# Modulation tiles of the first block as whole 128x2048 tiles in two neighbouring slots of the weight ring

## What is computed

```
mod = silu(c) @ w_mod + b_mod
shift, scale, gate = split(mod, 3)
h = rms_norm(x, g_pre) * (1 + scale) + shift
proj = h @ w_in
y = concat(attention, spatial gating, gated linear attention) * silu(z)
out = y @ w_out
x = x + gate * rms_norm(out, g_post)
```

## Time and profile before

| | |
|---|---|
| median of three runs | 2891.63 us |
| the profiled execution, its own time | 2893.03 us |
| span of its profile, first to last instruction | 2891.3 us |
| first block, about | 0 to 890 us |
| late modulation tiles on VectorE | 163 to 776 us |
| mean granted TensorE clock | 0.985 |
| TensorE busy | 2792.5 us (97%) |
| VectorE busy | 1792.4 us (62%) |
| ScalarE busy | 1375.3 us (48%) |
| late modulation transfers | 79 + 49 = 128 of 512 KB |

### The profile page before, as it was taken

The page is one execution under the profiler, slowest core; times in us unless marked ns, Lnnn a source line. Parts: engine busy times, 40 slices in busy tenths (PEclk is TensorE's granted clock), DMA queues, the critical chain, the costliest instruction groups (busy, mean ns, idle before and its releaser), DMA issues.

```text
span 2891.3 us, 35716 instructions
## 1 busy us (share of the span) xinstructions
PE 2792.5 (97%) x13338; PEld 2316.7 (80%) x13338; DVE 1792.4 (62%) x2196; ACT 1375.3 (48%) x1782; POOL 36.1 (1%) x69
## 2 busy tenths in 40 slices
PE   5799998999998999999999999999999999999998
PEld 4578786888887888888888888878888888888886
DVE  6889898768755565555445556575555545445565
ACT  4355445555544444453545444444545445545443
POOL 0000000000000000000000000000000000000000
PEclk8899999999999999999999999999999999999999
DMA  9977698875564555576555565645555765555664
GB/s 394 359 274 262 203 348 302 318 231 191 188 206 151 175 175 175 163 225 193 180 177 169 174 198 190 225 160 174 175 175 165 227 190 175 175 176 177 194 217 146
DMA packets 160199, 605.16 MB, mean 209 GB/s; under 512 B 18376, under 2 KB 18560, under 8 KB 154544
## 3 DMA queue, kind: packets, MB, share of 16 engines
q1 hardware_dynamic: 155376, 583.08, 60.3%
q0 software_dynamic: 4672, 19.98, 2.1%
HBM read 600.85 MB, written 2.14 MB: 209 GB/s over the span
## 4 chain that ended last, share of the span: by engine, by line
PE 67%; DVE 1%; DMA 0%; ACT 0%; issue 0%; SPq 0%; ACTq 0%; DVEq 0%
PE acc L780 62%; PE psT L728 2%; PE psS L761 1%; PE psS L751 1%; PE psT L734 1%; PE psS L768 0%; DMA raw<-in_w 0%; DVE wlo L434 0%; ACT whi L317 0%; DVE stage L543 0%; DVE x L487 0%; PE psT L724 0%; DVE stage L532 0%; DVE x L486 0%; DVE x L468 0%
## 5 line engine op out<-in xcount | busy, mean ns | idle before, releaser
L434 DVE TENSOR_TENSOR wlo<-raw,whi 128x1024 fp32r<-128x1024 f32 x672 | 822.4, 1225 | 867.6 <-ACT whi L317 866.0
L317 ACT ACTIVATE whi<-raw 128x1024 fp32r<-128x1024 f32 x672 | 711.2, 1059 | 996.5 <-PE acc L780 980.8
L780 PE MATMUL acc<-whi,xhi 128*128 128x512 f32 x2304 | 638.4, 398 | 2.4 <-DVE xlo L440 1.5
L780 PE MATMUL acc<-whi,xlo 128*128 128x512 f32 x2304 | 619.9, 390 | 0.0
L780 PE MATMUL acc<-wlo,xhi 128*128 128x512 f32 x2304 | 619.7, 390 | 0.0
L780 PEld LDWEIGHTS acc<-whi,xlo 128*128 128x128 f32 x2304 | 433.3, 188 | 92.5
L780 PEld LDWEIGHTS acc<-wlo,xhi 128*128 128x128 f32 x2304 | 433.3, 188 | 91.7
L780 PEld LDWEIGHTS acc<-whi,xhi 128*128 128x128 f32 x2304 | 423.5, 189 | 83.2 <-DVE xlo L440 3.0
L1412 ACT ACTIVATE whi<-raw 128x1024 fp32r<-128x1024 f32 x177 | 187.2, 1059 | 270.1 <-PE acc L2163 164.3
L2163 PE MATMUL acc<-whi,hhi 128*128 128x512 f32 x864 | 250.2, 412 | 40.7 <-DVE hlo L1645 40.7
L1634 DVE TENSOR_TENSOR wlo<-raw,whi 128x1024 fp32r<-128x1024 f32 x177 | 215.2, 1222 | 89.0 <-ACT whi L1412 88.0
(11 more groups left out here) (320 smaller groups left out, 2126.6 us busy)
## 6 DMA issues: line engine op xcount, KB each, us to landing
raw<-in_w SPq DMA_DIRECT2D x849, 512.0 KB, 3.5
raw<-in_w_late SPq DMA_DIRECT2D x79, 512.0 KB, 5.1
mraw<-in_w SPq DMA_DIRECT2D x63, 512.0 KB, 4.8
mraw<-in_w_late SPq DMA_DIRECT2D x49, 512.0 KB, 4.9
b_y<-in_w_early SPq DMA_DIRECT2D x12, 1024.0 KB, 10.8
mraw<-in_w_early SPq DMA_DIRECT2D x7, 1024.0 KB, 10.6
scr<-in_w_early SPq DMA_DIRECT2D x7, 1024.0 KB, 11.8
sgl<-in_w_early SPq DMA_DIRECT2D x6, 1024.0 KB, 13.6
```

The lines of the kernel that those rows point to most:

```text
L317: act.activation(whi[:, n % SLOTS, :], raw[:, n % SLOTS, :], ACT.Copy).then_inc(s_hi, 1)
L434: dve.tensor_tensor(wlo[:, n % SLOTS, :], raw[:, n % SLOTS, :], whi[:, n % SLOTS, :].bitcast(F32), ALU.subtract).then_inc(s_lo, 1)
L780: m = pe.matmul(acc[c % 2][:, tb, :], a[:, kk, tb * P:(tb + 1) * P], b[:, n % SLOTS, k * CW:(k + 1) * CW], start=(kk == 0 and q == 0), sto ...
```

## The change

- A late modulation tile is whole: 128x2048, 1 MB, one transfer and one VectorE sum. There are 64 instead of 128. `summed` is gone, `mcol` loses its last axis, and `mraw` keeps its size.
- In the ring such a tile takes two neighbouring slots. `ring_places()` gives each item its first slot, the count of its first slot's uses, and the item that was last in the top one of its slots. SyncE waits for that one. Weights still take one slot. A tile starts at an even slot, so an even number of weights lies between two tiles.
- `late_steps()` now has, in layer 0, the odd steps from 33 on but 63, 71, 77 and 119; in layer 1 steps 3, 5, ... 17 and then 21, 25, ... 81.
- R_GATE stays 68 in layer 0 and goes from 85 to 83 in layer 1.

```diff
-LATE = [(0, 2, kt, half) for kt in range(KT) for half in range(2)]
-LATE += [(1, third, kt, half) for kt in range(KT) for third in range(2) for half in range(2)]
-LATE += [(1, 2, kt, half) for kt in range(KT) for half in range(2)]
+LATE = [(0, 2, kt) for kt in range(KT)]
+LATE += [(1, third, kt) for kt in range(KT) for third in range(2)]
+LATE += [(1, 2, kt) for kt in range(KT)]
-R_FULL = (62, 63, 64, 70, 71, 77, 99, 119)
+R_FULL = (63, 71, 77, 119)
...
-    steps = [(0, r) for r in range(R_RING, GRAN1) if r not in R_FULL]
-    steps += [(1, 1 + i) for i in range(16)]
-    steps += [(1, 21 + 2 * i) for i in range(32)]
+    steps = [(0, r) for r in range(R_RING + 1, GRAN1, 2) if r not in R_FULL]
+    steps += [(1, 3 + 2 * i) for i in range(8)]
+    steps += [(1, 21 + 4 * i) for i in range(16)]
...
-R_GATE = [[r for (layer, r), i in LATE_AT.items() if i == GATED[l]][0] + 2 for l in range(DEPTH)]
+R_GATE = [[r for (layer, r), i in LATE_AT.items() if i == GATED[l]][0] + 3 - l for l in range(DEPTH)]
...
+def ring_places():
+    places, last, uses = {}, {}, [R_RING // SLOTS if i < SLOTS else 0 for i in range(RING)]
+    at_slot = 0
+    for item in ITEMS:
+        first, width = at_slot % RING, ring_width(item)
+        assert first % width == 0
+        uses[first] += 1
+        places[item] = first, uses[first], last.get(first + width - 1)
+        for i in range(first, first + width):
+            last[i] = item
+        at_slot += width
+    return places, last
...
-            if k >= RING:
-                sp.wait_ge(*consumed(ITEMS[k - RING]))
+            if before:
+                sp.wait_ge(*consumed(before))
...
-            _, third, kt, part = LATE[i]
+            _, third, kt = LATE[i]
             dve.wait_ge(*landed(("m", i)))
-            dve.scalar_tensor_tensor(out=slot(("m", i)), in0=slot(("m", i)), scalar=1.0,
-                                     in1=crow[:, part * MOD_W:(part + 1) * MOD_W], op0=ALU.mult, op1=ALU.mult,
-                                     accum_out=mcol[:, third, kt, part:part + 1]).then_inc(s_macc, 1)
+            dve.scalar_tensor_tensor(out=slot(("m", i)), in0=slot(("m", i)), scalar=1.0, in1=crow[:], op0=ALU.mult,
+                                     op1=ALU.mult, accum_out=mcol[:, third, kt:kt + 1]).then_inc(s_macc, 1)
...
-                summed(0, kts)
-                summed(1, kts)
```

More of the change, by code:

```diff
@@ L997, in ring_items, with ring_width @@
     return out
+def ring_width(item):
+    return 2 if item[0] == "m" else 1
+def ring_places():
[10 more added lines that the diff above has]
+    return places, last
 ITEMS = ring_items()
-ITEM = {item: k for k, item in enumerate(ITEMS)}
+PLACES, LAST_USE = ring_places()
 def ring_slot(item):
-    if item in ITEM:
-        return ITEM[item] % RING
-    return item[1] % SLOTS
+    return PLACES[item][0] if item in PLACES else item[1] % SLOTS
 def ring_uses(item):
-    if item in ITEM:
-        return ITEM[item] // RING + 1 + (R_RING // SLOTS if ITEM[item] % RING < SLOTS else 0)
-    return item[1] // SLOTS + 1
+    return PLACES[item][1] if item in PLACES else item[1] // SLOTS + 1
 def h_fill(l, r):
@@ L1103, in first_block @@
     crow = sb("crow", [P, D])
-    mraw = sb("mraw", [P, 2, MOD_W])
+    mraw = sb("mraw", [P, 2, GK * CW])
     gain = sb("gain", [P, D])
@@ L1130, in first_block @@
     sinks = sb("sinks", [P, A_HEADS])
-    mcol = sb("mcol", [P, 3, KT, 2])
+    mcol = sb("mcol", [P, 3, KT])
     mbias = sb("mbias", [P, DEPTH, 3, KT])
@@ L1300, in slot @@
     def slot(item):
-        i = ring_slot(item)
-        return raw[:, i, :] if i < SLOTS else mraw[:, i - SLOTS, :]
+        i, width = ring_slot(item), ring_width(item)
+        tile = raw[:, i:i + width, :] if i < SLOTS else mraw[:, i - SLOTS:i - SLOTS + width, :]
+        return tile.rearrange("p a n -> p (a n)")
     def landed(item):
@@ L1326, in weights, with item @@
             sp.dma_start(slot(("w", n)), dram["w1"][n]).then_inc(s_w[n % SLOTS], 16)
-        def item(k):
-            kind, i = ITEMS[k]
-            if k >= RING:
-                sp.wait_ge(*consumed(ITEMS[k - RING]))
-            elif k < SLOTS:
-                sp.wait_ge(*split(R_RING - SLOTS + k))
+        def item(name):
+            kind, i = name
+            first, _, before = PLACES[name]
+            top = first + ring_width(name) - 1
+            if before:
+                sp.wait_ge(*consumed(before))
+            elif top < SLOTS:
+                sp.wait_ge(*split(R_RING - SLOTS + top))
             else:
@@ L1337, in item @@
             src = dram["w1"][i] if kind == "w" else dram["w_late"][i]
-            sp.dma_start(slot(ITEMS[k]), src).then_inc(s_w[k % RING], 16)
+            sp.dma_start(slot(name), src).then_inc(s_w[first], 16)
         for tb in range(TB):
@@ L1353, in _ @@
                 weights(n)
-        for k in range(len(ITEMS)):
-            item(k)
+        for name in ITEMS:
+            item(name)
         for n in range(SLOTS if s_next else 0):
-            sp.wait_ge(*consumed(ITEMS[max(k for k in range(len(ITEMS)) if k % RING == n)]))
+            sp.wait_ge(*consumed(LAST_USE[n]))
             sp.dma_start(raw[:, n, :], dram["w"][n]).then_inc(s_next[n], 16)
@@ L1652, in tile @@
             dve.scalar_tensor_tensor(out=big[n % len(big)], in0=big[n % len(big)], scalar=1.0, in1=crow[:], op0=ALU.mult,
-                                     op1=ALU.mult, accum_out=mcol[:, third, kt, 0:1]).then_inc(s_macc, 1)
+                                     op1=ALU.mult, accum_out=mcol[:, third, kt:kt + 1]).then_inc(s_macc, 1)
         def late(i):
-            _, third, kt, part = LATE[i]
+            _, third, kt = LATE[i]
             dve.wait_ge(*landed(("m", i)))
-            dve.scalar_tensor_tensor(out=slot(("m", i)), in0=slot(("m", i)), scalar=1.0,
-                                     in1=crow[:, part * MOD_W:(part + 1) * MOD_W], op0=ALU.mult, op1=ALU.mult,
-                                     accum_out=mcol[:, third, kt, part:part + 1]).then_inc(s_macc, 1)
-        def summed(third, kts):
-            link(dve.tensor_tensor(mcol[:, third, kts, 0], mcol[:, third, kts, 0], mcol[:, third, kts, 1], ALU.add))
+            dve.scalar_tensor_tensor(out=slot(("m", i)), in0=slot(("m", i)), scalar=1.0, in1=crow[:], op0=ALU.mult,
+                                     op1=ALU.mult, accum_out=mcol[:, third, kt:kt + 1]).then_inc(s_macc, 1)
         def columns_of(l, j):
@@ L2213, in modulation_stream @@
     w = w_mod.reshape(DEPTH, D, 3, KT, P).transpose(0, 2, 3, 4, 1)
-    late = [w[l, third, kt, :, part * MOD_W:(part + 1) * MOD_W] for l, third, kt, part in LATE]
+    late = [w[l, third, kt] for l, third, kt in LATE]
     return {"w_early": np.ascontiguousarray(w[0, 0:2]), "w_late": np.stack(late)}
```

8 lines of the change are left out of this document (3 added, 5 removed).

## The result

The changed kernel takes **2905.44 us** (median of six runs, 2900.48 to 2913.2), the kernel before beside it 2891.51 us (six runs, 2889.99 to 2893.78). The ratio is 1.0048, 95% interval 1.0038 to 1.0059: slower by 11 to 17 us, where 2891.6 us and a range up to 2898 had been forecast. The profiled execution is 2908.0 us with a span of 2906.3 us.

The account below looks back on a forecast made before the run. TensorE was taken to bound the first block, hiding VectorE and transfers behind its weight lead. Every term was worth 0, so the profiled 2893.03 us stayed the same; for the median, 2891.6 us, range 2888.5 to 2898.

Parts of the forecast that it names:

- What bounds the kernel: First block: TensorE bound wherever late modulation tiles lie; smallest weight lead 1.70 us, at granule 97 of layer 0.
- Order in the ring: Granules 96 and 97, layer 0: paired weight requests shift the lead, 2.9 us more to 3.1 less; no stall taken.
- The loop: Rival: ring closes too slowly between granules 96 and 118; 2895 to 2904 us, most likely 2898; chance 0.15.
- Transfers: Modulation tiles in the ring: same bytes in 64 fewer pieces, rate margin from about 1% to 9%; worth 0.
- The rival by which the rows are cut into the same pieces: Transfers stay at 388 GB/s, time as forecast; no chance of its own, within the 0.79 shared with forecast and small stalls.
- A blocking sum: VectorE's 2.29 us sum delays the even granule's `lo`, but `wlo` is needed only in a granule's last third; worth 0.
- VectorE's relief: Whole sums save VectorE 17.5 us busy time, worth 0; rival that it is felt at "go": 2885.6 us, chance 0.06.
- Change of layer: TensorE's 10.6 us wait for normalised x between layers: no VectorE backlog enters the chain; worth 0.
- go: TensorE's 4.65 us wait for a `psT` bank: chain starts at its own gate transpose, step 68, unchanged; worth 0.
- hlo: TensorE's waits for `hlo` before 156 us and early in layer 1: worth 0, at most a few tenths.
- the gate of layer 1: Gate moved from step 85 to 83 on TensorE; bank read with 3.8 us of cover; worth 0.

Follow-up runs that it names:

- pairs of halves: Kernel before with its half transfers and half sums, but two at each of the changed kernel's steps, gate of layer 1 at step 83: 2899.17 us, ratio 1.0022.
- the gate at 85: Changed kernel with the gate transposed at step 85 in both layers: 2900.46 us, ratio 1.0031 to the kernel before.
- the three sums moved: Changed kernel with three VectorE modulation sums later (steps 53 to 54, 61 to 63, 67 to 68), ring order unchanged: 2904.82 us, ratio 1.0043 to before.

## Why the prediction was wrong

**What bounds the kernel.** That TensorE's lead is what counts was right. That the smallest lead of the kernel before decides was wrong: a lead of 1.7 us is a stock, and the question is whether the ring refills it. Before, it did: the lead is 3.2 us at granule 112.

**Order in the ring, "I take no stall": the step that failed.** The requests went out as forecast. Granule 97 starts 5.8 us later than before, and its pair of weights was requested at 409.59, so 403.8 in the time of before (forecast 403.2 and 403.5). The `whi` of granules 96 and 97 in the changed kernel, ScalarE, and the first matmuls of 96, TensorE:

```profile
417.99 1.06 ACT L1431 ACTIVATE whi<-raw 128x1024 fp32r<-128x1024 f32 x1 [5.36 <-DMA raw<-in_w]
420.20 1.07 ACT L1431 ACTIVATE whi<-raw 128x1024 fp32r<-128x1024 f32 x1 [1.15 <-PE acc L2174]
```
```profile
420.05 1.07 PE L2174 MATMUL acc<-whi,hhi 128*128 128x512 f32 x4
```

The lead at 97 is 422.76 - 421.27 = 1.5 us, hardly less than 1.7, but for another reason than forecast: the earlier request gained nothing, since the weight was there about 10 us after it, against 9 before. And the even granule, of which the prediction said that it "has more to lose", lost nearly all: at 96 the lead is 420.05 - 419.05 = 1.0 us instead of 5.1, at 98 it is 0.5 and at 100 there is none left. I had weighed one granule where I should have followed the round.

The loop stood among the rivals at a chance of 0.15, and three terms of it were mis-sized. It goes over six granules and holds both flights, the modulation tile's and the weight's (7.2 and about 6.7 us); I had closed it over four, with one. The loop over four is there too: with the flight of 6.7 us it comes to 5.2 + 6.7 = 11.9 us against 10.88, 0.5 us too slow for a pair of granules, where the loop over six is 0.88 too slow. The flight of the second weight was put at 4.8 to 6.6 us and expected to fall, "a loop that waits empties its own queue". It did not. Transfers of the changed kernel, 420 to 491 us, as the earlier trace rows:

```profile
raw<-in_w SPq DMA_DIRECT2D x16, 512.0 KB, 6.1
raw<-in_w_late SPq DMA_DIRECT2D x7, 1024.0 KB, 6.9
```

6.1 us instead of 5.3; that of the second weight, 6.7, was just above the upper end. And the loss is 0.74 us in each of eleven pairs, 8.2 us, not 0.9 in six loops less the lead, 3.7. The clock, to which I had given up to 1.4 us in each of six loops, took nothing there (1.00 in all three stretches).

The Trainium skill (DMA: Bandwidth & Descriptors, section Anatomy of one DMA) fits the time of one transfer issued from GpSimd as 2.0 us plus bytes over 436 GB/s. The estimate worked out from it, that a weight behind another would land 4.4 us after its request, does not hold in this filled queue of SyncE, where it took 6.7; the trace decides.

**Transfers, "the margin grows from about 1% to as much as 9%".** The rate fell from 388 to 340 GB/s, and the share from 1.01 to 0.93. What a full queue can carry says nothing when the requests come late. The rival by which the rows are cut into the same pieces is out too: there are 160199 packets before and 150982 now, as a row of 8 KB is one packet where it had been two of 4 KB. The small packets had been no limit: the pairs of halves have 160200 of them and lose nothing in the ring.

**"A blocking sum ... Worth 0."** Wrong: 4.0 us in layer 0 and 1.4 in layer 1, where the pairs of halves lost 3.1 and 2.2. Without the first four granules of layer 1, whose time differs from execution to execution, it is 1.1 and 1.2 us there. About 1.5 of the 4.0 is granted clock that fell behind the `psT` wait (0.91 in 300 to 320); with the tiles of 97 to 117 left out it stayed at 1.00 there, and 33 to 68 lost 2.5. I named what stands behind the sum as `lo`, and did not go on to the steps where VectorE also reads `psS` and `psT`. The rule of the prediction itself, who waits for what is queued behind, was used on one instruction of several.

**VectorE's relief, 17.5 us, worth 0.** Right in worth. The busy time fell by 6.6 us: most of the 5.2 us of accumulator reads had lain within the time of their neighbours (read at 448.41 for 0.08 us, the sum's own end at 448.48), and neighbours overlap by 0.07 us, once less for each sum that is gone.

**Change of layer, worth 0.** Wrong by 1.3 us. VectorE had no backlog, as said; ScalarE had.

**"go", `hlo`, the gate of layer 1, worth 0.** Right: 4.7 us as before, no wait at step 86 of layer 1.

## What to carry to other kernels

In this ring of few slots a larger piece lengthened the round. So follow one slot from request to request, with every flight and every instruction in it, over as many steps as it takes to close, and compare that with the consumer's pace for those steps. A lead in one place does not answer this. And before two short instructions on a nearly full engine are joined or lumped at one step, list all that stands behind them there, above all reads that free a PSUM bank for TensorE; busy time saved on an engine that is not the bound was worth nothing here, while the same edit's latency was paid for.

## What was not expected of the hardware

- TensorE's granted clock stayed 1.00 from 420 to 480 us, through six waits of 0.2 to 1.7 us that lie 6 to 17 us apart. After one wait of 0.95 us and a fill it fell in the changed kernel, at granule 66: the first four matmuls took 1.86 us (309.56 to 311.42) instead of 1.04, and the stretch has 0.91. The same wait of 0.95 us did the same with the gate at 85, and did not with the tiles of 97 to 117 left out. The pairs of halves waited 1.31 us at the same fill and kept 1.00. And the ring is not safe from it: with the three sums moved, after waits of 1.02 and 1.96 us at 448 and 456 us, the stretch 440 to 460 has 0.93. What decides was not found.
- The same instructions ahead of granule 33 ended up to 5.4 us apart in twelve executions, so one profile of each kernel tells the total to some us only, while the ring's stretch came out at 59.84 us in four kernels.
